# Splitting each 288-column expert matmul into two of 144 columns on the same stationary weights

## The chip, the cores and the metric

One NeuronCore of one Trainium2 chip runs the whole kernel. The metric is device time in microseconds (us), lower is better; the number that counts is the median of several executions. One execution was also recorded by the hardware profiler, and all rows below are from it.

## The reference, cut to what matters

A two-layer encoder on 1024 tokens of 1024 features, in float32. Layer 0 has attention and a dense SwiGLU, layer 1 a gated spatial mixing and a top-2-of-8 expert SwiGLU. The edit is in a helper of all the large products, but acts only in the expert part:

```python
logits = (xt @ w_router).astype(jnp.float32)
top_val, top_idx = lax.top_k(logits, TOP_K)          # 2 of 8 experts for each token
hg = lax.ragged_dot(xs, w_gate_e, sizes)             # 1024 -> 3584
hu = lax.ragged_dot(xs, w_up_e, sizes)               # 1024 -> 3584
ys = lax.ragged_dot(jax.nn.silu(hg) * hu, w_down_e, sizes)   # 3584 -> 1024
```

## The kernel before, in words

A float32 product is made of three products of float32r halves. Every operand is kept as a high part and the remainder: `wh` and `wl` for the weights, `exh` and `exl` (both in the tile `ex`) for the gathered tokens, `mah` and `mal` for the hidden activations. `product` (L333) issues the three terms high*high, high*low and low*high into one PSUM region. Each term is one `pe.matmul` whose stationary operand is a 128x128 weight tile and whose moving operand has `n` columns, one per token. Only where `n` is 512 and `wide` isn't set does it cut a term into two matmuls of 256 columns, with the same stationary operand. A few first products have hand-made cuts: `EVEN` cuts one term of a 512-column product at 320, and items of 256 columns cut one term at 192. In the trace every `pe.matmul` shows as two instructions, a LDWEIGHTS (row PEld) and a MATMUL (row PE).

The expert part works through items, an item being one expert with its tokens, padded to one of the widths 384, 304, 288, 256 or 240 (`WIDTHS`). The list of items is made on the chip. In this trace there are one item of 304, two of 288, two of 256 and three of 240 columns, in that order. `by_width` has one loop for each width, and in it `item_pe` (L2541 and on) issues an item on TensorE: `gate_up_pe` (L1383) with 28 hidden tiles x 2 matrices x 8 blocks of the contraction x 3 terms = 1344 matmuls; for widths above 256 then `down_pe` (L1440) twice, each with 14 units x 2 x 4 x 3 = 336 matmuls, with transposes of the next item's tokens (`turn_x_pe`, L2418) and of the results (`rows_y_pe`, L2448) between them. Items of at most 256 columns use `down_rows_pe`, where the 512 columns of the weights move instead; items of 240 also have their own gate and up routine (L2494, L2495).

Weight units of 512 KB are loaded by SP into four buffers of `wraw`; ScalarE makes `wh` (L324) and VectorE makes `wl` (L328). They count what TensorE has used in `unit_used` and what is ready in `lo_done`, and the inner loops run over four units, so TensorE waits at most once in 24 terms. The spatial mixing of layer 1 has another pattern that the argument uses: it alternates a matmul of 256 columns (L1994) with one of 128 columns (L1995), each with its own 128x128 stationary tile in float32r.

Of the kernel before, what the change touches and what calls it, by code (L numbers as in the profile page):

```python
# [60 lines left out]
def build(nc, io):  # L61
    ctx = ExitStack()
    with ctx:
# [265 lines left out]
                              ALU.subtract).then_inc(lo_done, 1)  # L329

        COLS = 256

        def product(pe, out, a_hi, a_lo, b_hi, b_lo, first, last, wide=False, cuts=None):  # L333

            n = b_hi.shape[-1]
            for part in range(3):
                a, b = ((a_hi, b_hi), (a_hi, b_lo), (a_lo, b_hi))[part]
                w = COLS if n == 2 * COLS and not wide else n
                edges = [*cuts, n] if cuts and part == 0 else [*range(0, n, w), n]
                for c, d in zip(edges[:-1], edges[1:]):  # L340
                    s = slice(c, d)
                    mm = pe.matmul(out[:, s], a, b[:, s], start=first and part == 0 and c == 0,  # L342
                                   stop=last and part == 2 and d == n)
            return mm
# [293 lines left out]
        def values_pe(pe):  # L638
            for g in range(2):
                xh, xl, x_first = ((rsh, rsl, 0), (xs[:, 1, 0], xs[:, 1, 1], KD))[g]  # L640
                for j in range(4):
                    pe.wait_ge(lo_done, j + 1)
                    for kk in range(2):
                        k = 2 * j + kk
                        pe.wait_ge(n_lo, x_first + k + 1)
                        for t in range(4 * g, 4 * g + 4):
                            c = slice(t % 4 * P, t % 4 * P + P)
                            w = slice(512 * kk, 512 * kk + 512)
                            if g == 1 and k == 0 and t == 4 + SPREAD[1] % 4:
                                pe.wait_ge(n_rstd, 1)  # L650
                            if g == 1 and k == 0 and t == 4 + SPREAD[0] % 4:
                                pe.wait_ge(n_rstd, 2)
                            mm = product(pe, bank(t), xh[:, k, c], xl[:, k, c], wh[:, j, w], wl[:, j, w],
                                         k == 0, k == KD - 1, wide=True)
                            if k == KD - 1 and t < 4 * g + 3:
                                mm.then_inc(v_mm, 1)
                        if g == 1 and kk == 1 and j < 3:
                            mm.then_inc(unit_used, 1)
                        elif kk == 1 and j == 3:
                            mm.then_inc((v_mm, unit_used)[g], 1)  # L660
                        if g == 0 and k == 1:
                            pe.wait_ge(setup_in, 48)
                            pe.matmul(bank(6)[0:8, 0:EXT_B], t5s[:], onehot[:], start=True, stop=True).then_inc(t5_mm, 1)
                        if g == 0 and k == 4:
                            start_sums_pe(pe, 1)
                        if g == 0 and k == 5:
                            pe.wait_ge(ext_ready, 4)
                            start_spread_pe(pe, 1)
                        if g == 0 and k == 6:
                            start_sums_pe(pe, 0)  # L670
                        if g == 0 and k == 7:
                            start_spread_pe(pe, 0)

        def half_pe(pe, u, half, b, ks, used=1, ready=None):

            for k in ks:
                if ready:
                    ready(k)
                mm = product(pe, bank(b), wtile(wh, u % 4, k), wtile(wl, u % 4, k), xs[:, half, 0, k], xs[:, half, 1, k], k == 0, k == KD - 1)
            if KD - 1 in ks:  # L680
                if half == 0:
                    mm.then_inc(first_half, 1)
                else:
                    mm.then_inc(unit_used, used)
# [392 lines left out]
        def out_unit_pe(pe, q, j, half, b, ready=None, order=tuple(range(KD)), kick=False):  # L1077
            pe.wait_ge(lo_done, 4 * q + j + 1)
            for i, k in enumerate(order):
                if ready:  # L1080
                    ready(i)
                mm = product(pe, bank(b), wtile(wh, j, k), wtile(wl, j, k), xs[:, half, 0, k], xs[:, half, 1, k],
                             i == 0, i == KD - 1, cuts=EVEN if kick and i == 0 else None)
            return mm
# [1391 lines left out]
        def paired(n):  # L2476
            return 2 * n < 2 * COLS

# [541 lines left out]
```

## Time and profile before

| | |
|---|---|
| median of 3 runs | 3488.38 us (3488.0 to 3492.32) |
| the profiled execution, its own time | 3493.34 us |
| its span in the trace | 3491.8 us |
| TensorE matmul (PE) busy | 3442.3 us, 99% of the span, 25495 matmuls |
| TensorE weight load (PEld) busy | 3243.7 us, 93%, 25495 loads |
| VectorE (DVE) busy | 2043.4 us, 59% |
| ScalarE (ACT) busy | 1563.0 us, 45% |
| mean granted TensorE clock | 0.993 |

The mean duration of one matmul in the trace is its latency, from its record's start to its modelled end, and successive matmuls overlap. What a matmul costs in a stream is the distance from one start to the next, so stretches with a known count of matmuls are read, not the means.

### The profile page before, as it was taken

To read this page: it belongs to the slowest core of one execution; us is meant where nothing else is said; L and a number is where in the kernel's file an instruction comes from. 1 tells how busy PE (TensorE), PEld (TensorE's weight loads), DVE (VectorE), ACT (ScalarE), POOL (GpSimd) and SP (SyncE) were. 2 spreads that over 40 slices of the span, in tenths; PEclk is the share of its full clock that TensorE was granted. 3 is DMA by queue.
4 is the path that set the end of the run, shared out by engine and by line. 5 is a ranking of instruction groups with operands and counts; after the bars stand their busy time and mean duration, and the time that the engine had idled before them with its cause. 6 is when DMAs were issued, how large, how long until landed. Compare 5 with 4: busy or idle time off the path is not lost.

```text
span 3491.8 us, 68944 instructions
## 1 busy us (share of the span) xinstructions
PE 3442.3 (99%) x25495; PEld 3243.7 (93%) x25495; DVE 2043.4 (59%) x3129; ACT 1563.0 (45%) x2335; POOL 221.4 (6%) x259
## 2 busy tenths in 40 slices
PE   9999899999999999999999999999999999999998
PEld 8888799999999899799999999999999898898886
DVE  6455577766544556454455455446555587686774
ACT  4455433333333433354344344445454465554653
POOL 1000000000100000022010001001010020010100
PEclk9999899999999999999999999999999999999999
DMA  5111332222553423266455445456566575665654
GB/s 199 38 51 41 137 117 73 85 83 84 200 186 117 137 67 110 105 201 182 152 183 193 163 164 200 164 168 228 192 223 207 187 244 195 202 231 190 228 198 155
DMA packets 159181, 548.23 MB, mean 157 GB/s; under 512 B 23345, under 2 KB 23353, under 8 KB 159056
## 3 DMA queue, kind: packets, MB, share of 16 engines
q1 hardware_dynamic: 123248, 444.67, 38.8%
q0 software_dynamic: 32352, 95.54, 7.8%
q10 hardware_dynamic: 3456, 6.29, 0.5%
q8 instruction: 86, 1.41, 0.2%
q14 instruction: 39, 0.32, 0.0%
HBM read 508.20 MB, written 59.08 MB: 162 GB/s over the span
## 4 chain that ended last, share of the span: by engine, by line
PE 96%; DVE 2%; ACT 1%; issue 1%; DMA 0%; DVEq 0%; SPq 0%; POOL 0%; POOLq 0%; ACTq 0%
PE ps L342 77%; PE ps L2494 8%; PE ps L2495 4%; PE ps L738 1%; PE ps L809 1%; PE ps L821 1%; PE ps L2418 1%; PE ps L839 0%; PE ps L829 0%; ACT eA L878 0%; DMA yT<-in_xT 0%; PE ps L762 0%; PE ps L1207 0%; PE ps L1994 0%; PE ps L2448 0%
## 5 line engine op out<-in xcount | busy, mean ns | idle before, releaser
L328 DVE TENSOR_TENSOR wl<-wraw,wh 128x1024 fp32r<-128x1024 f32 x800 | 979.3, 1225 | 887.1 <-ACT wh L324 878.0
L324 ACT ACTIVATE wh<-wraw 128x1024 fp32r<-128x1024 f32 x796 | 841.0, 1057 | 930.0 <-PE ps L342 867.1
L342 PE MATMUL ps<-ex,wh 128*128 128x256 f32 (+2 forms) x4484 | 850.7, 289 | 1.1 <-DVE wl L328 1.1
L342 PEld LDWEIGHTS ps<-ex,wh 128*128 128x128 f32 x4484 | 704.4, 188 | 1.5 <-issue 1.4
L342 PE MATMUL ps<-ex,wl 128*128 128x288 f32 (+2 forms) x2240 | 647.1, 289 | 0.0
L2494 PE MATMUL ps<-ex,wh 128*128 128x480 f32 x1344 | 445.2, 382 | 0.0
L342 PEld LDWEIGHTS ps<-ex,wl 128*128 128x128 f32 x2240 | 420.6, 188 | 0.0
L342 PE MATMUL ps<-xs,wh 128*128 128x256 f32 x2432 | 388.9, 282 | 4.3 <-DVE qAl L865 1.9
L342 PE MATMUL ps<-bc,wh 128*128 128x256 f32 (+1 forms) x2496 | 386.6, 277 | 0.0
L2495 PE MATMUL ps<-ex,wl 128*128 128x240 f32 x1344 | 366.5, 273 | 0.0
L342 PEld LDWEIGHTS ps<-xs,wh 128*128 128x128 f32 x2432 | 327.0, 190 | 15.9 <-issue 9.9
L342 PEld LDWEIGHTS ps<-bc,wh 128*128 128x128 f32 x2496 | 330.9, 188 | 0.5 <-issue 0.5
L2494 PEld LDWEIGHTS ps<-ex,wh 128*128 128x128 f32 x1344 | 252.0, 187 | 41.7
L2495 PEld LDWEIGHTS ps<-ex,wl 128*128 128x128 f32 x1344 | 254.8, 190 | 0.1
L342 PE MATMUL ps<-bc,wl 128*128 128x256 f32 x1248 | 243.7, 277 | 0.0
L342 PE MATMUL ps<-xs,wl 128*128 128x256 f32 x1216 | 240.0, 279 | 0.0
L342 PE MATMUL ps<-wl,mah 128*128 128x512 f32 x560 | 219.8, 392 | 0.0
L342 PE MATMUL ps<-wh,mal 128*128 128x512 f32 x560 | 219.7, 392 | 0.0
L342 PE MATMUL ps<-wh,mah 128*128 128x512 f32 x560 | 219.0, 391 | 0.0
L342 PE MATMUL ps<-act_hl,wh 128*128 (+2 forms) x1408 | 218.5, 277 | 0.0
L342 PE MATMUL ps<-mah,wh 128*128 (+2 forms) x672 | 200.1, 298 | 0.0
L342 PE MATMUL ps<-mah,wl 128*128 (+2 forms) x672 | 199.8, 297 | 0.0
(390 smaller groups left out, 4773.9 us busy)
## 6 DMA issues: line engine op xcount, KB each, us to landing
wraw<-in_w_expert SPq DMA_DIRECT2D x676, 512.0 KB, 3.3
wraw<-in_w_main SPq DMA_DIRECT2D x164, 512.0 KB, 3.8
act_d<-ast POOLq DMA_DIRECT2D x22, 512.0 KB, 2.9
araw<-act_d POOLq DMA_DIRECT2D x22, 512.0 KB, 5.1
hT<-h_d POOLq DMA_DIRECT2D x4, 2048.0 KB, 14.3
h_d<-hT POOLq DMA_DIRECT2D x3, 2048.0 KB, 9.6
hT<-in_xT POOLq DMA_DIRECT2D x2, 2048.0 KB, 9.6
xrow_d<-rows ACTq DMA_DIRECT2D x16, 256.0 KB, 2.1
```

The costliest lines, as they stand in the source:

```text
L324: act.activation(wh[:, j], wraw[:, j], ACT.Copy).then_inc(hi_done, 1)
L328: dve.tensor_tensor(wl[:, j], wraw[:, j], wh[:, j].bitcast(F32), ALU.subtract).then_inc(lo_done, 1)
L342: mm = pe.matmul(out[:, s], a, b[:, s], start=first and part == 0 and c == 0, stop=last and part == 2 and d == n)
L738: mm = pe.matmul(ps[:, starts[h] + a * P:starts[h] + b * P], (qAh, qAh, qAl)[part][hp, tc], key, start=part == 0, stop=part == 2)
L809: mm = pe.transpose(ps[:, o:o + P], eA[:, h, kk * P:kk * P + P], ident[:])
L821: mm = pe.matmul(Y_OUT[h * HD:h * HD + HD], v, ptA[:, kk, h], start=kk == 0, stop=kk == na - 1)
L2418: mm = pe.transpose(bank(banks[k], P, P * s_), xg[:, s_, k * P:k * P + P], ident[:])
L2494: pe.matmul(o.rearrange("p (c t) -> p c t", c=2), wtile(wh, j, k), ex[:, :, k, 0:n], start=k == 0, stop=False)
L2495: mm = pe.matmul(o[:, 0:n], wtile(wl, j, k), ex[:, 0, k, 0:n], start=False, stop=k == KD - 1)
```

## The change

In `product`, a term of 288 columns is issued as two matmuls of 144 columns. The stationary operand, the order of the three terms and the PSUM region are the same. The `start` flag stays on the first half of the first term, the `stop` flag on the second half of the last.

```diff
         COLS = 256
+        TWIN = 288
 
         def product(pe, out, a_hi, a_lo, b_hi, b_lo, first, last, wide=False, cuts=None):
 
             n = b_hi.shape[-1]
             for part in range(3):
                 a, b = ((a_hi, b_hi), (a_hi, b_lo), (a_lo, b_hi))[part]
-                w = COLS if n == 2 * COLS and not wide else n
+                w = COLS if n == 2 * COLS and not wide else TWIN // 2 if n == TWIN else n
                 edges = [*cuts, n] if cuts and part == 0 else [*range(0, n, w), n]
                 for c, d in zip(edges[:-1], edges[1:]):
                     s = slice(c, d)
```

## Rows read from the trace of the kernel before

**Rows 1.** The page: the chain that ended last, by engine and by line.
```profile
PE 96%; DVE 2%; ACT 1%; issue 1%; DMA 0%; DVEq 0%; SPq 0%; POOL 0%; POOLq 0%; ACTq 0%
```

**Rows 2.** Stretches (start:end, length, busy us and count by engine, clock, DMA): the two items.
```profile
1780.53:2056.91 276.38, 274.95 (x2068) 273.98 (x2066) 138.86 (x166) 118.94 (x162) 15.82 (x14) 1.00 0.53 177
2056.91:2333.28 276.37, 274.94 (x2067) 273.98 (x2066) 138.86 (x166) 118.83 (x162) 16.55 (x14) 1.00 0.52 176
```

**Rows 3.** Stretches of TensorE alone: the 288-column products, three parts per item.
```profile
1780.53:1959.80 179.27, 179.27 (x1347) 1.00 0.56 187
1959.80:2004.61 44.81, 44.81 (x338) 1.00 0.49 164
2009.40:2055.63 46.23, 45.23 (x340) 1.00 0.46 151
...
sum 540.62, PE 538.63; mean PE 89.77
```

**Rows 4.** Instruction groups by form, both items: matmuls and their weight loads.
```profile
L342 PE MATMUL ps<-ex,wh 128*128 128x288 f32 x1792 | 358.6, 296 | 0.0
L342 PE MATMUL ps<-ex,wl 128*128 128x288 f32 x896 | 264.8, 295 | 0.0
```

**Rows 5.** Instruction groups by form, whole trace: matmuls and loads of 512-column products in halves.
```profile
L342 PE MATMUL ps<-bc,wl 128*128 128x256 f32 x1248 | 243.7, 277 | 0.0
L342 PEld LDWEIGHTS ps<-bc,wl 128*128 128x128 f32 x1248 | 188.3, 188 | 0.0
```

**Rows 6.** Timeline of the weight loads where one 256-column term is cut at 192.
```profile
2335.99 0.41 PEld L342 LDWEIGHTS ps<-ex,wh 128*128 128x128 f32 x3
2336.32 0.19 PEld L342 LDWEIGHTS ps<-ex,wl 128*128 128x128 f32 x1
```

**Rows 7.** Timeline of the matmuls at the same place.
```profile
2335.76 0.39 PE L342 MATMUL ps<-ex,wh 128*128 128x256 f32 x2
2335.99 0.28 PE L342 MATMUL ps<-ex,wl 128*128 128x256 f32 x1
2336.10 0.50 PE L342 MATMUL ps<-ex,wh 128*128 128x192 f32 x3
2336.44 0.28 PE L342 MATMUL ps<-ex,wl 128*128 128x256 f32 x1
```

**Rows 8.** Timeline of the weight loads, 256 and 128 columns in turn.
```profile
1307.11 0.19 PEld L1995 LDWEIGHTS ps<-ws,vgl 128*128 128x128 f32 x1
1307.23 0.19 PEld L1994 LDWEIGHTS ps<-ws,vgh 128*128 128x128 f32 x1
1307.34 0.19 PEld L1995 LDWEIGHTS ps<-ws,vgl 128*128 128x128 f32 x1
...
1308.03 0.19 PEld L1995 LDWEIGHTS ps<-ws,vgl 128*128 128x128 f32 x1
```

**Rows 9.** The chain in order of time (start, us): back-to-back transposes, 128 columns each.
```profile
2008.34 1.31 PE ps L2448 x12
```

**Rows 10.** Waits in the two items: who waited for whom, us, times, longest.
```profile
DVE wl L328 <- ACT wh L324: 246.2, 160, 3.6
ACT wh L324 <- PE ps L342: 202.9, 108, 3.2
PE ps L2448 <- DVE ybuf L2686: 2.0, 2, 1.0
```

**Rows 11.** Stretches with fewer or shorter matmuls (columns as in rows 2).
```profile
381.00:391.00 10.00, 7.29 (x77) 5.50 (x73) 7.69 (x21) 7.69 (x16) 0.00 (x0) 1.00 0.00 0
366.00:376.00 10.00, 10.00 (x68) 8.36 (x69) 5.56 (x18) 4.67 (x10) 0.00 (x0) 0.52 0.57 222
1467.00:1477.00 10.00, 9.59 (x107) 9.10 (x107) 7.95 (x51) 8.30 (x16) 0.68 (x1) 1.00 0.56 211
```

**Rows 12.** Timeline: a burst of transposes before the first item.
```profile
1486.64 5.26 PE L2418 MATMUL ps<-ident,xg 128*128 128x128 f32 x24 [7.06 <-issue]
```

**Rows 13.** The same burst as a stretch (columns as in rows 2).
```profile
1486.64:1491.60 4.96, 4.96 (x24) 4.96 (x25) 3.32 (x6) 3.71 (x7) 4.89 (x3) 0.50 0.98 369
```

## The prediction

> **What bounds the kernel now.** I read the chain of waits first: 96% of it is TensorE [rows 1], so a change that acts on TensorE acts on the end. The next question is what in TensorE sets the pace, and a busy share of 99% doesn't tell, because overlapped latencies count as busy. So I went to the stretches. The two items of 288 columns take 276.4 us each at a granted clock of 1.00 [rows 2]. In each of them the changed products fill three stretches, gate and up (1344 matmuls) and the two halves of down (336 each); over both items these are 4032 matmuls in 540.6 us [rows 3] (the second item's three stretches have the same lengths, and the counts in the rows hold a few neighbours more). That is 0.1341 us from one matmul to the next. The 0.296 us in the groups by form [rows 4] is the latency, and dividing the items by it would be wrong by more than a factor of two.
>
> VectorE and ScalarE are no rivals for the bound here: they are busy 139 and 119 us of 276 [rows 2], and ScalarE itself waits 203 us for TensorE to free weight buffers, VectorE in turn 246 us for ScalarE [rows 10]. TensorE waits only 2.0 us in both items, twice 1.0 us for VectorE's copy of results.
>
> **The change part by part.** It takes away 4032 matmuls of 288 columns and puts 8064 of 144 in their place. The columns that stream are the same, so nothing is saved there except, at best, a little fixed time. No other width is touched: no other product of this run has 288 moving columns, and VectorE, ScalarE and the DMAs issue what they did. The whole question is whether the second half brings a second weight load, and what the load costs when only 144 columns stream over it.
>
> First, is there a second load? The kernel already cuts 512-column terms into halves with the same stationary tile, and there each matmul of 256 columns has a load of its own, 1248 for 1248 [rows 5]. Nothing is merged, so I count 8064 loads instead of 4032.
>
> Second, how often can loads follow each other? While 256 or 288 columns stream, the load lies under the stream and its cost can't be seen. It shows where matmuls are short. One place has almost the form of this change: a 256-column term cut into 192 and 64 columns on the same weights [rows 6, 7]. Three loads, for the 192, the 64 and the next 256 columns, start at 2335.99 and on, and the load behind them at 2336.32, so 0.33 us for three, 0.110 each. The matmuls tell the same: the uncut pair of the term before takes 2335.99 - 2335.76 = 0.23 us, the cut one 2336.44 - 2336.10 = 0.34 us for the same 512 columns. The cut alone costs 0.11 us, a whole load, although 64 columns need far less. Another place has 256 and 128 columns in turn [rows 8]: from 1307.11 to 1308.03 there are eight intervals of loads, 0.115 each, where 192 columns on average would stream in 0.085 by the pace of 256 columns in 0.113 (three of them from 2335.76 to 2336.10 in rows 7). So with short matmuls a float32r load of 128 columns sets the pace, at 0.110 to 0.115 us. A third row gives the pace of an even stream: 12 transposes with 128 moving columns and a load each take 1.31 us [rows 9], 0.109 each. It is the nearest in column count (128 to 144) and evenness, though its data are float32 in transposes, so that it isn't a pure test of the load. The mixed stream of rows 8 is slower since a load there also waits for a long matmul to start; in the changed stream all matmuls are alike. I take 0.109.
>
> Third, the sum. 8064 x 0.109 = 879.0 us. The 2.0 us that TensorE waits for VectorE's copies stays (it lies at the ends of the down halves, where the last result must be there whatever came before). 879.0 + 2.0 - 540.6 = **340.4 us more**. Per term that is 0.218 us for two halves against 0.134 us for one. Per item it is 276.4 + 170.2 = 446.6 us. Nothing hides it, because TensorE is on the chain all through both items; nor does anything get back time later, since all items behind are bound by TensorE's own pace too. What the longer items give to the others is only slack: ScalarE waits longer for `unit_used`, and weights arrive earlier relative to their use.
>
> The base: the profiled execution took 3493.3 us (span 3491.8 and 1.5 around it), 5.0 us above the median of the runs shown. The difference of 340.4 is between stretches of the same execution, so I add it to the median: 3488.4 + 340.4 = 3828.8, rounded to **3829 us**. On the profiled execution it would be 3834.
>
> The bounds of the unknown cost. From below, a cadence of 0.108, a little under what rows 9 can have been rounded from, gives 8064 x 0.108 + 2.0 - 540.6 = 332 us more, 3821 us. From above, the pace of the mixed stream, 0.115 to 0.1155, gives 8064 x 0.1155 + 2.0 - 540.6 = 393 us more, 3881 us. Below nothing is excluded by the two places where a short matmul was seen to pay a whole load, unless 144 columns behave unlike 64 and 128.
>
> A rule of the Trainium skill speaks against this size. "TensorE: Matmul & The Clock Gate", section on the back-to-back issue gap, gives about 81 ns per matmul for a sustained stream of load and matmul pairs with 128 columns. By it the changed items would cost 8064 x 0.081 = 653 us instead of 541, an estimate from that page of 114 us more with the same 2.0 us of waits, 3602 us. The trace doesn't agree with that rule: its streams with 128-column stationary tiles and short matmuls stand at 109 ns [rows 9] and 115 ns [rows 8].
>
> **The rivals.**
>
> *The load is partly hidden.* Loads could run beside the stream more than the cut terms show, say because a uniform stream lets them be issued further ahead. Halfway between the load's 0.109 and the pure stream of 144 columns, 0.113 x 144/256 = 0.064, is 0.0865: 8064 x 0.0865 + 2.0 - 540.6 = 159 us more, 3647 us. Against it: in rows 8 the distance stays at 0.115 over eight loads, without catching up. The skill's figure of 81 ns belongs to this case. Chance 4%.
>
> *The load is wholly hidden or not repeated* (the other side). If the second half finds its weights already in place, or loads can follow each other in under 0.067 us, the stream alone counts: two halves cost 2 x 0.064 = 0.128 against 0.134, which is 8064 x 0.064 + 2 - 540.6 = 23 us less, 3466 us; if each matmul has a few ns of its own that the split doubles, it is level. It speaks for it that a 288-column matmul costs 0.134 where 0.113 x 288/256 = 0.127 would be proportional, so the wide form is somewhat dear. It decides from a load cadence of 0.067 on, and rows 6 and 7 show 0.110 on a cut of the same kind, with the same weights. Chance 3%, faster and level in about equal parts.
>
> *The clock falls.* TensorE would stream only 288 columns in 0.218 us, about 0.113 x 288/256 / 0.218 = 58% of the time. The kernel has a stretch with the granted clock at 0.52 [rows 11], nearly all of it at the lower of the two levels of 1.2 and 2.4 GHz. At 0.50 [rows 13] a burst of 24 transposes with loads took 5.26 us, 0.219 each [rows 12], twice 0.109. If it stayed low in both items: 8064 x 0.219 + 2 - 540.6 = 1227 us more, 4716 us; with a tenth of the matmuls at it, 806 x 0.110 = 89 us above my forecast, 3918 us. Against it: in 10 us with 107 mostly short matmuls the clock was 1.00, as in a stretch where TensorE was busy only 7.3 of 10 us [rows 11], and the burst at 0.50 stood behind 7.06 us of idle time [rows 12], which the new loop doesn't have. Chance 6%.
>
> *Instructions come late.* The loop bodies double in instructions, and TensorE would wait for its own program. The pairs of the dense layer have a loop body of 336 matmuls (2 x 7 x 4 x 3 x 2), against 192 in the new ones, and show no idle time before them [rows 5]. Each us per turn of a loop (four units, 96 terms, 42 turns or so in both items) would add 42 us: 3871. Chance 3%, inside the range.
>
> **How the numbers follow.** The load-bound case has 84% (0.108 to 0.1155 us each); with it and the late instructions the range 3815 to 3885 holds some 87%, a little less than is left after the clock's 6% and the two hidden cases' 7%. I leave it as it is, since its ends are the bounds of the one unknown cost. The measurement can tell about 0.2% of the time, 7 us, from no change. Slower by more than that: load-bound 84, partly hidden 4, clock 6, late instructions 3, together 97%, less one for what I haven't thought of: 96%. Within 0.2%: 2%. Faster: 2%.
>
> **What would show it.** In the trace of the changed kernel: 29527 matmuls and as many loads (25495 + 4032); the two items at about 447 us each, with starts of loads 0.109 apart and no gap between them; the weight loads nearly as busy as the matmuls in these stretches; all other stretches of their old length; the granted clock at 1.00 in both items; ScalarE's wait for TensorE up by some 300 us. The prediction is wrong if loads are fewer than matmuls, if their starts are under 0.1 us apart, if the clock is near 0.5 anywhere in these items, or if the items of other widths change as well.

## The result and the profile after

The changed kernel takes 4196.16 us (median of 6 runs, 4193.14 to 4198.29) against 3489.31 us before (6 runs), a ratio of 1.2023 with a 95% interval of 1.2007 to 1.2038. It is slower, as forecast, but by 706.9 us instead of 340.4.

The page of the changed kernel: the span, the engines' busy times, and the span in 40 slices.

```profile
span 4191.6 us, 77200 instructions
...
PE 4137.7 (99%) x29527; PEld 3940.4 (94%) x29527; DVE 2044.6 (49%) x3129; ACT 1565.3 (37%) x2335; POOL 221.8 (5%) x259
...
PEclk9999999999999999999996555555999999999999
```

Matmuls and loads went up by 4032 each, the number forecast, and VectorE and ScalarE do what they did. New is the row of the granted clock: in seven slices it is at or near half.

The same stretches as in [rows 2], the two items of 288 columns, and the item of 256 behind them (start:end, length, busy us and count of PE, PEld, DVE, ACT, POOL, then clock, DMA).

```profile
1773.90:2231.71 457.81, 456.39 (x4083) 455.44 (x4081) 139.33 (x166) 118.80 (x162) 14.66 (x14) 1.00 0.31 107
2231.71:3033.09 801.38, 797.70 (x4082) 797.16 (x4081) 139.60 (x166) 118.85 (x162) 14.38 (x14) 0.55 0.18 61
3033.09:3264.44 231.35, 231.35 (x1701) 217.44 (x1700) 133.17 (x160) 114.76 (x157) 16.78 (x14) 1.00 0.62 207
```

Two items with the same work differ by 343.6 us. The first went up by 181.4 us, near the 170 of the forecast, the second by 525.0. Together that is 706.4 us, the 706.9 of the medians within their scatter, and the item behind them is as it was. (The two profiled executions differ by 699.8 us in span, because in the changed one everything before the items took 6.6 us less, 1773.90 against 1780.53. The edit doesn't touch that part.) So there are two things to explain: 181 us per item, and the second item's excess. The second item cut by the clock:

```profile
2234.46:2236.41 1.95, 1.95 (x17) 1.95 (x18) 0.00 (x0) 0.00 (x0) 1.61 (x2) 1.00 1.10 288
2236.41:2953.20 716.79, 716.79 (x3362) 716.79 (x3362) 114.41 (x138) 100.84 (x142) 11.29 (x11) 0.50 0.17 57
2953.20:3033.09 79.89, 78.79 (x705) 78.42 (x704) 22.66 (x25) 18.01 (x21) 0.00 (x0) 1.00 0.27 93
```

For 716.8 us TensorE ran at the lower of its two levels (1.2 of 2.4 GHz), without a moment of idle time: 3362 matmuls, 0.2132 us each. In the gate and up part of the first item, at 1.00, it is 0.1117 each (below). 3362 x (0.2132 - 0.1117) = 341 us. What happened just before the fall, in the timeline of the changed kernel's TensorE:

```profile
2230.35 1.53 PE L2449 MATMUL ps<-ident,ybuf 128*128 128x128 f32 x12 [0.99 <-DVE ybuf L2687]
2234.46 0.66 PE L343 MATMUL ps<-ex,wh 128*128 128x144 f32 x4 [2.59 <-DVE wl L328]
```

Between the last transposes of the first item and the first product of the second TensorE idled 2.59 us. The kernel before has no such gap: there the products go on as the transposes end.

```profile
2055.63 1.53 PE L2448 MATMUL ps<-ident,ybuf 128*128 128x128 f32 x12 [0.99 <-DVE ybuf L2686]
2056.91 0.52 PE L342 MATMUL ps<-ex,wh 128*128 128x288 f32 x2
```

The profile puts the gap down to VectorE's `wl`, which ran from 2233.03 to 2234.25. But in the kernel before the same unit was made only from 2058.30 on, when the products had been going for 1.4 us. They didn't need it, so the label was a suspect rather than an answer. Another candidate was the instructions. The DMA view of the changed kernel from 2231 to 2235 us, 40 slices of 0.1 us:

```profile
GB/s 0 0 0 0 0 0 164 0 0 0 0 0 0 0 0 0 0 0 0 0 0 0 0 0 0 0 0 0 0 0 0 0 287 328 451 410 410 369 328 492
...
q8 instruction: 1, 0.02, 1.4%
```

One 16 KB packet of instructions goes out at 2231.6, as the last transpose starts, about when TensorE jumps back to the top of its item loop. The profile doesn't name the engine whose instructions a packet holds. Counting that queue over whole second items gives nothing in the kernel before. In the changed one it is:

```profile
q8 instruction: 10, 0.16, 0.1%
```

**Theory A**, from this: with a new matmul and load for each half term, the body of the item loop no longer stays in TensorE's instruction memory. The jump back costs a fetch and a pause of 2.6 us. The clock falls after the pause, and a stream of 144-column pieces doesn't get it back. **Rivals**: B, such a stream loses the clock at a hand-over with or without a pause; C, it needs the fetch itself or is chance; D, any stream, also the dense one of whole 288-column matmuls, would have stayed low. For the 181 us per item, the load as the pace stood against rival E, a fixed time for each matmul.

### The profile page after: what moved, and what is told of

Its sections match the earlier page's. It is cut to its first block, busy times and chain, and to the rows that moved or that the text cites. A ratio compares the mean times of both kernels' runs of the same rounds, so it can differ in the third digit from the quotient of the medians.

```text
span 4191.6 us, 77200 instructions
## 1 busy us (share of the span) xinstructions
PE 4137.7 (99%) x29527; PEld 3940.4 (94%) x29527; DVE 2044.6 (49%) x3129; ACT 1565.3 (37%) x2335; POOL 221.8 (5%) x259
## 4 chain that ended last, share of the span: by engine, by line
PE 96%; DVE 1%; ACT 1%; issue 1%; DMA 0%; DVEq 0%; SPq 0%; POOL 0%; POOLq 0%; ACTq 0%
PE ps L343 81%; PE ps L2495 7%; PE ps L2496 4%; PE ps L739 1%; PE ps L810 1%; PE ps L2419 1%; PE ps L822 1%; PE ps L840 0%; ACT eA L879 0%; PE ps L830 0%; PE ps L1208 0%; DMA yT<-in_xT 0%; PE ps L763 0%; PE ps L1995 0%; DVE wl L328 0%
## 5 line engine op out<-in xcount | busy, mean ns | idle before, releaser
L343 PE MATMUL ps<-ex,wh 128*128 128x144 f32 (+2 forms) x6276 | 1236.9, 319 | 3.8 <-DVE wl L328 3.8
L343 PEld LDWEIGHTS ps<-ex,wh 128*128 128x128 f32 x6276 | 1087.5, 230 | 4.3 <-issue 4.2
L343 PE MATMUL ps<-ex,wl 128*128 128x144 f32 (+2 forms) x3136 | 836.3, 319 | 0.0
L343 PEld LDWEIGHTS ps<-ex,wl 128*128 128x128 f32 x3136 | 632.5, 230 | 0.0
L2495 PEld LDWEIGHTS ps<-ex,wh 128*128 128x128 f32 x1344 | 252.0, 187 | 41.6
L343 PE MATMUL ps<-mah,wh 128*128 (+2 forms) x1120 | 268.1, 309 | 0.1
L343 PE MATMUL ps<-mal,wh 128*128 (+2 forms) x1120 | 267.9, 308 | 0.0
L343 PE MATMUL ps<-mah,wl 128*128 (+2 forms) x1120 | 267.9, 308 | 0.0
L2496 PEld LDWEIGHTS ps<-ex,wl 128*128 128x128 f32 x1344 | 254.8, 190 | 0.1
L1418 ACT ACTIVATE mst<-ps 128x256 f32<-128x256 f32 (+2 forms) x140 | 56.6, 404 | 457.9 <-PE ps L343 426.5
```

Source lines behind the costliest of these rows:

```text
L1418: act.activation(buf[:, par, 0:n], bank(b + par, n), ACT.Silu).then_inc(silu_done, 1)
L2495: pe.matmul(o.rearrange("p (c t) -> p c t", c=2), wtile(wh, j, k), ex[:, :, k, 0:n], start=k == 0, stop=False)
L2496: mm = pe.matmul(o[:, 0:n], wtile(wl, j, k), ex[:, 0, k, 0:n], start=False, stop=k == KD - 1)
```

## The experiments

**Two copies of the item's code.** TensorE's code for 288 columns is written out once for the first item and once more for the later ones, so that the second item is reached without a jump back.

```diff
             for i, w in enumerate(WIDTHS):
...
+                if w == TWIN and frm == 1:
+                    m0, m1 = eng.to_reg(c0), eng.to_reg(c1)
+                    mid = eng.to_reg(c0 + 1)
+                    with eng.If_lt(m0, c1):
+                        with nc.Fori(c0, c0 + 1, engines=[eng.engine]) as it:
+                            item(it, w)
+                    with eng.If_lt(mid, c1):
+                        with nc.Fori(c0 + 1, c1, engines=[eng.engine]) as it:
+                            item(it, w)
+                    continue
```

> The changed kernel, with TensorE's code for the 288-column items written out twice, once for the first and once for the later ones, so that the second item is reached by going on and not by a jump back over a loop body that has become twice as long. Theory A (the 2.6 us of idle TensorE at the second item's start is its program being fetched again, and this pause makes the clock fall): no instruction fetch and no 2.6 us gap there, granted clock 1.00 in both items, 458 us for each, 3489 + 2 x 181 = 3851 us. Rival B (a stream that is half loads loses the clock by itself at some hand-over, whatever the pause): clock low in the second item as in the changed kernel, 4190 to 4200 us.

Measured: 3850.54 us, ratio 1.1035 (1.1017 to 1.1054). The two items:

```profile
1773.33:2231.06 457.73, 456.32 (x4084) 455.44 (x4081) 139.24 (x166) 118.49 (x162) 14.52 (x14) 1.00 0.32 107
2231.06:2688.79 457.73, 456.31 (x4083) 455.44 (x4081) 139.27 (x166) 118.39 (x162) 14.28 (x14) 1.00 0.32 106
```

No gap, no fall, 346 us less than the changed kernel with the same products. The first product starts at 2231.06, and VectorE begins the `wl` unit in question only at 2232.45, so the gap wasn't a wait for it. Instructions are still loaded in the second item (8 packets), but ahead of their use. B falls.

**Control: two copies in the kernel before.** The same edit with whole 288-column matmuls.

> Control: the kernel before, with TensorE's code for the 288-column items written out twice as in the run with two copies. By every theory nothing changes, 3489 us within 0.2%. If the two copies themselves cost or gain something, the differences read against runs with two copies have to be corrected by it.

Measured: 3490.2 us, ratio 1.0003 (0.9994 to 1.0013). The copies cost nothing.

**Two copies and a pause by a semaphore.** At the start of a 288-column item:

```diff
             f0 = it * NF_E + F0
+            if n == 288:
+                pe.wait_ge(lo_done, 4 * q + 4)
```

> As the run with two copies, but at the start of every 288-column item TensorE waits until all four weight units of the first turn are ready, which by the trace of the changed kernel ends 2.6 us after the last transposes: a pause of the same size made by a semaphore. Theory A (a pause of that size is enough): the clock falls at the start of one or both items, 4190 us with one item at the low clock, up to 4530 us with both. Rival C (it was the fetch as such, or chance): clock 1.00, 3851 + 5 = 3856 us.

Measured: 4538.87 us, ratio 1.3004 (1.2978 to 1.303): the upper end, both items. TensorE's waits at the two starts in the timeline, and the first item from the fall on:

```profile
1779.14 0.66 PE L343 MATMUL ps<-ex,wh 128*128 128x144 f32 x4 [2.70 <-DVE wl L328]
...
2580.71 0.66 PE L343 MATMUL ps<-ex,wh 128*128 128x144 f32 x4 [2.70 <-DVE wl L328]
```

```profile
1781.00:2497.80 716.80, 716.80 (x3363) 716.80 (x3362) 114.30 (x138) 100.84 (x142) 10.79 (x11) 0.50 0.17 57
```

A pause of 2.70 us made without any fetch gives the same fall, 1.9 us after the products begin, and the same low stretch of 716.8 us. C falls.

**The same pause in the kernel before**, one loop and whole matmuls.

> The kernel before (288 columns in one matmul) with the same wait at the start of the 288-column items. Theory A with its second half (the dense stream of 288 columns gets the clock back within some us, the stream of 144-column pieces can't): two pauses of 2 to 3 us and at most some 10 us of low clock after each, 3489 + 5 to 3489 + 25 us. Rival D (whatever the stream, a clock lost at an item's start stays low for hundreds of us): 3489 + 270 us or more.

Measured: 3498.11 us, ratio 1.0021 (1.0011 to 1.0031). From the start of the first 288-column item:

```profile
1781.30:1785.30 4.00, 3.96 (x18) 3.96 (x19) 0.00 (x0) 0.00 (x0) 1.53 (x2) 0.58 0.91 292
1785.30:2057.00 271.70, 271.24 (x2036) 270.27 (x2034) 134.85 (x159) 117.18 (x159) 12.89 (x11) 1.00 0.52 173
```

The clock falls here too, and is back after 3.4 us, at the second item as well (low from 2061.8 to 2065.2). The stream of whole matmuls recovers; D falls.

**The changed kernel and a dense burst.** After the first turn of each 288-column item, 32 more matmuls with 288 moving columns.

```diff
                 mm.then_inc(unit_used, 1)
+                if n == TWIN and isinstance(u, int) and u == 1 and up:
+                    for _ in range(32):
+                        pe.matmul(bank(7, n), x[0][:, 0, 0:P], x[0][:, 0, 0:n], start=True, stop=True)
```

> The changed kernel, with 32 more matmuls of 288 columns (float32r, into a PSUM bank that nothing reads then) after the first turn of each 288-column item; they are extra work and leave the output as it is. Theory A (a dense stream gives the clock back): in the second item the clock rises during or right after the burst, at most 30 us after its start; the low stretch shrinks from 717 us to about 50, total 3489 + 362 + 13 for the bursts + about 20 = 3885 us. Rival D (the low clock doesn't depend on how dense the stream is): it stays low through the item, 4196 + 13 = 4209 us.

Measured: 3884.94 us, ratio 1.1133 (1.1114 to 1.1151). The second item before the burst, the burst's first part, its rest, and the products behind it:

```profile
2242.20:2280.60 38.40, 38.40 (x182) 38.40 (x182) 4.50 (x5) 5.38 (x7) 0.44 (x1) 0.50 0.21 71
...
2280.60:2283.00 2.40, 2.40 (x12) 2.40 (x12) 1.44 (x2) 2.08 (x3) 0.00 (x0) 0.50 0.00 0
2283.00:2286.00 3.00, 3.00 (x25) 3.00 (x24) 0.61 (x2) 0.35 (x2) 0.00 (x0) 1.00 0.54 156
2286.00:2720.00 434.00, 433.50 (x3878) 432.62 (x3876) 128.73 (x152) 108.98 (x148) 11.80 (x11) 1.00 0.32 103
```

Fetch, pause and fall are as in the changed kernel, but 2.4 us into the burst the clock is back, and the 144-column stream behind it keeps it. Some 10 us of extra work save 311 us.

**A shorter pause**: two copies, TensorE waits for VectorE's last addition instead.

```diff
+            if n == 288:
+                pe.wait_ge(hg_ok, 6 * it + YS0)
```

> Two copies of the item code, and at the start of each 288-column item TensorE waits for VectorE's last addition of the item before, by the traces a pause of about 1.5 us instead of 2.6. Theory A says nothing of the size: if 1.5 us is too short, clock 1.00 and 3851 + 3 = 3854 us; if it is enough at one of the two starts about 4190 us, at both about 4530 us.

Measured: 4199.33 us, ratio 1.2036 (1.2012 to 1.206). TensorE waited at both starts, and the clock fell at the first alone:

```profile
1781.60 0.66 PE L343 MATMUL ps<-ex,wh 128*128 128x144 f32 x4 [1.58 <-DVE hg L2586]
```

```profile
2581.97 0.66 PE L343 MATMUL ps<-ex,wh 128*128 128x144 f32 x4 [1.59 <-DVE hg L2586]
```

```profile
1784.00:2500.80 716.80, 716.80 (x3363) 716.80 (x3362) 115.15 (x139) 101.74 (x143) 11.17 (x12) 0.50 0.17 57
2582.00:3038.00 456.00, 455.02 (x4068) 454.14 (x4068) 136.49 (x162) 117.42 (x161) 14.28 (x14) 1.00 0.33 107
```

1.6 us is at the edge: the same wait was followed by a fall once and not the other time, in one execution. The other execution took as long (4198.89 us), which fits one low item too. What else enters isn't settled. A pause of about 1 us with transposes beside it, which each item has in all these kernels, never did it while 144-column pieces ran.

**Half the dose.** Only gate and up in halves, then only down, both with the one loop of the changed kernel; the edit is a flag that `gate_up_pe` or `down_pe` hands to `product`.

```diff
-                w = COLS if n == 2 * COLS and not wide else TWIN // 2 if n == TWIN else n
+                w = COLS if n == 2 * COLS and not wide else TWIN // 2 if twin and n == TWIN else n
```

> The changed kernel with its one loop, but only the gate and up products (2688 of 4032 terms) in two matmuls, the down products whole. At full clock 2688 x (0.2234 - 0.1334) = 242 us more, 3731 us. The loop body then lies between those of the two kernels. If it still stays in the instruction memory, no fetch and no pause at the second item: 3731 us. If not: pause, low clock through the second gate and up part (1344 x 2 x 0.1016 = 273 us more), and back soon after the whole 288-column matmuls of the down part begin: about 4005 us.

> The other half of the dose: the changed kernel with its one loop, only the down products (1344 of 4032 terms) in two matmuls, gate and up whole. At full clock 1344 x (0.2234 - 0.134) = 120 us more, 3609 us. If the loop body is too long and is fetched again at the second item, a pause of 2.6 us comes there, but the whole 288-column matmuls of gate and up follow it and give the clock back within some us: 3609 + 3 + 3 = 3615 us. Rival D (a lost clock stays lost for hundreds of us): 3609 + about 270 us.

Measured: 3730.47 us, ratio 1.0691 (1.0673 to 1.0709), and 3614.31 us, ratio 1.0359 (1.034 to 1.0377). With gate and up alone there was no gap and no fall. The gate and up part of its second item:

```profile
2176.26:2476.34 300.08, 300.08 (x2690) 300.08 (x2689) 96.41 (x120) 82.98 (x120) 15.46 (x14) 1.00 0.34 112
```

For down alone, instruction packets in the first and the second item, and the second item's start:

```profile
q8 instruction: 7, 0.11, 0.2%
```

```profile
q8 instruction: 9, 0.15, 0.2%
```

```profile
2118.60 0.84 PE L343 MATMUL ps<-ex,wh 128*128 128x288 f32 x2 [2.62 <-DVE wl L328]
```

```profile
2118.60:2121.70 3.10, 3.10 (x13) 3.10 (x14) 0.00 (x0) 0.00 (x0) 1.57 (x2) 0.50 1.00 275
```

Over the four kernels with one loop: the first item loads 4 packets in the kernel before, 6 with gate and up in halves, 7 with down in halves, 8 with both, and the second item loads 0, 0, 9 and 10. So a body whose first pass loads 6 packets stays, and one whose first pass loads 7 doesn't. These counts are not the exact length of the body: where it is fetched again, the second pass loads two more than the first. With down alone the fetch, the pause and the fall are all there, but gate and up follow with whole 288-column matmuls, and the second item takes 4.2 us more than the first (341.04 against 336.84), instead of 344.

**Three pieces of 96 columns**, on two copies (`TWIN // 3` in place of `TWIN // 2`).

> Two copies of the item code as in the run before, and every 288-column term in three matmuls of 96 columns. If one 128-column load per matmul sets the pace (0.1117 us), a term costs 0.335 us: 3489 + 4032 x 0.335 - 541 + 2 = 4301 us at full clock. Rival E (the cost of a cut is a fixed time per matmul beside the stream, (0.2234 - 0.120) / 2 = 0.052 us): 3 x 0.052 + 0.120 = 0.276 us per term, 4063 us. The clock may fall here without a pause, since only 36% of the time streams; then more than 4301 us, and the loads at 0.213 us where the granted clock is low.

Measured: 5524.93 us, ratio 1.583 (1.5803 to 1.5856). Loads at the start of the first item, then the part that streams at the low clock:

```profile
1777.02 0.75 PEld L343 LDWEIGHTS ps<-ex,wh 128*128 128x128 f32 x6
1777.69 0.41 PEld L343 LDWEIGHTS ps<-ex,wl 128*128 128x128 f32 x3
1778.03 0.75 PEld L343 LDWEIGHTS ps<-ex,wh 128*128 128x128 f32 x6
```

```profile
1782.00:2633.20 851.20, 851.20 (x3992) 851.20 (x3992) 93.81 (x116) 82.96 (x120) 10.61 (x11) 0.50 0.12 39
```

At full clock 9 loads in 1.01 us, 0.112 each, as with 144 columns; at half clock 851.2/3992 = 0.213, again as with 144. The columns don't matter, the load sets the pace, and E (0.092 each) falls. Here the clock fell 4.2 us after the item's start without any pause beyond the usual 1.03 us. It came back during the next transposes and fell again 5.1 us after the products went on (at 2854.81), with no pause at all:

```profile
2853.00:2859.90 6.90, 6.89 (x62) 6.66 (x60) 4.67 (x7) 1.91 (x4) 0.00 (x0) 0.99 0.26 78
2859.90:4146.70 1286.80, 1285.80 (x6029) 1285.65 (x6029) 133.66 (x155) 115.42 (x156) 14.08 (x14) 0.50 0.11 37
```

So a stream of pieces this short doesn't even keep the clock.

**Half of the stationary columns.** Two copies; the second matmul of a term takes 64 of the 128 stationary columns unless it opens or closes an accumulation, so that half the output rows lack that part.

```diff
+                    m = P // 2 if n == TWIN and c and not (first and part == 0) and not (last and part == 2) else P
-                    mm = pe.matmul(out[:, s], a, b[:, s],
+                    mm = pe.matmul(out[0:m, s], a[:, 0:m], b[:, s],
```

> Two copies of the item code, two matmuls of 144 columns per term, but of the second ones all that neither open nor close an accumulation (3696 of 4032) take only 64 of the 128 stationary columns and leave the other half of the output rows without that term. The moving columns are as before. If the load sets the pace, its time goes with the stationary columns: a pair costs 0.112 + 0.056 = 0.168 us, 3851 - 3696 x 0.056 = 3644 us. Rival E (a fixed time per matmul whatever it loads): 3851 us.

Measured: 3686.63 us, ratio 1.0567 (1.0545 to 1.0588). Gate and up of the first item:

```profile
1776.48:2023.18 246.70, 246.70 (x2690) 246.70 (x2688) 96.33 (x120) 83.09 (x120) 14.19 (x14) 1.00 0.41 136
```

With the same moving columns 164 us less than with full loads, 0.044 for each narrow one, where a load that halves exactly would give 0.056. E, by which nothing would have changed, stays down. In this stretch 1232 of the 1344 second matmuls are narrow; each saves (300.12 - 246.70)/1232 = 0.043 us and is left with 0.068. That is more than half a load, but also what 144 columns take to stream by the pace of the kernel before, 0.1341/2 = 0.067. With 0.067 for each narrow one the sum would have been 3850.5 - 3696 x 0.0447 = 3685 us, where 3686.6 were measured. So the run may have met the stream and not the load, and it doesn't tell how long a narrow load takes.

## Why the prediction was wrong

The bound, the count and the load: right. TensorE is the path through both items, the second load is there for every half (29527 of each), and a load of 128 stationary columns sets the pace. The gate and up part of the first item, which answers to the first of [rows 3]:

```profile
1773.90:2074.02 300.12, 300.12 (x2691) 300.12 (x2689) 96.41 (x120) 83.15 (x120) 14.66 (x14) 1.00 0.33 113
```

That is 300.12/2688 = 0.1117 us each. I had taken 0.109 from the transposes [rows 9]; the cut term with 0.110 [rows 6] and the mixed stream with 0.115 [rows 8] lie on either side. The term was too small by 8064 x 0.0027 = 22 us: 340.4 + 22 = 362, and the version with two copies measured 361.5 above its kernel before. The figure of 81 ns per matmul at 128 columns, which the Trainium skill gives in "TensorE: Matmul & The Clock Gate", section on the back-to-back issue gap, does not hold here: 111.7 at 144 columns and 112 at 96, in float32r. By the same page's section on LDWEIGHTS, time goes with the stationary columns, 64/1.2 = 53 ns for half a tile as an estimate; the narrow matmul here took 68, near the 67 of its stream, so no run here tests that figure.

The step that failed is the clock, at 6%, and in it the sentence that the low burst stood behind idle time "which the new loop doesn't have". It does have it, once, and that one pause of 2.6 us was enough. I priced the low clock for a tenth of the matmuls (89 us above the forecast) or for all (1227 us above the kernel before, which is 887 above the forecast). It was 3362 of 8064, 42%, and 341 us, with the pause 344. The price of one matmul at the low clock, 0.219, came from a burst whose time in [rows 12] includes the latency of its last matmul; the stream showed 0.2132.

The pause itself stood among the rivals as late instructions, at 3%, but in the wrong place and with the wrong price. I asked whether TensorE can keep up inside a loop of 192 matmuls, and it can. I didn't ask whether the whole body of the item loop stays at hand for the jump back, and didn't count its instructions. Above all I kept the two as separate cases with small chances, where one brings on the other: 2.6 us of waiting cost 341 us of clock. The evidence against the clock rival was read too widely as well. The stretches with short or few matmuls at 1.00 [rows 11] tell that such a stream can keep a clock that it has. They don't tell that it gets back one that it lost, and this is where the time went.

What was right of the signs: nothing behind the two items changed (231.35 us for the 256-column item, where 231.32 were before), VectorE's and ScalarE's work was the same, and the changed kernel was slower. Of the signs of being wrong, the clock near 0.5 inside the items came. Two small readings were off as well, without weight in the sum: TensorE's idle time in both items before was 2.9 us by [rows 2], not 2.0 (the rest lies before the transposes between the parts and stayed), and the time by the 81 ns rule is 3603 us, not 3602. The range of 3815 to 3885 holds the version without the pause, 3850.54, and not the changed kernel. No version here beats the kernel before.

## What to carry to other kernels

Cutting a matmul on the same stationary tile brings a whole second load: as long as the pieces stream for less than a load takes (0.112 us for 128 float32r columns here), each piece costs a load, at 96 columns as at 144. Before making a loop body longer, look at how many instruction packets its first pass loads and whether its second pass loads any, since the cost of a jump back shows nowhere inside the body. And where pieces that wait for their loads make up the stream, price every pause of 1.6 us or more by how long the clock may stay low behind it; a short dense burst, or no pause, is cheap beside that.

## What the runs showed that was not expected

- A stream of 144-column pieces kept the higher clock for over 450 us and, having lost it, kept the lower for 716.8 us, the same to a tenth of a microsecond in the changed kernel and in the two with a pause by semaphore. It came back while the next item's 24 transposes ran (they began at 2949.59 in the changed kernel, the clock rose at 2953.2). All six long low stretches that reached such transposes, here and in the runs with the pauses and with three pieces, ended 2.5 to 4.6 us after these began. The same stream runs at either level; what came before decides. That the transposes brought the clock back is read from the times and wasn't tried.
- 288-column matmuls got it back in 3.4 us after the same kind of pause, 32 of them set into the thin stream in 2.4 us.
- Pieces of 96 columns lose the clock with no pause. Pauses of 2.6 to 2.75 us made it fall each time, seven in all, 1.6 us in one case of two.
- An item loop whose first pass loaded 7 or 8 instruction packets of 16 KB was fetched again on the jump back and cost 2.6 us at the start of the second pass; loops with 4 or 6 were not. That these packets are TensorE's is inferred from edits to its code alone that changed the counts.
